# The fourth sample part ahead of the sixth slot's low halves, and the first output slot ahead of two pooling maps

## The reference, cut to what matters

```python
hn = _rmsnorm(h, norm1_g[l])
u = hn @ w_in[l]                      # 1024 -> 512 (pooling) + 2 * 512 (convolution)
pool_out, _ = _pool_mixer(...)        # windowed means of 2, 4, 8, 16 minus token, a 128x128 map for each of 4 groups, scale
conv_out, _ = _conv_module(...)       # GLU, depthwise convolution of 31 taps, LayerNorm, SiLU, 512x512 pointwise
h = h + jnp.concatenate([pool_out, conv_out], axis=-1) @ w_out[l]
hn = _rmsnorm(h, norm2_g[l])
h = h + (_swiglu(hn, ...) if l % 2 == 0 else _moe(hn, ...))
```

## Time and profile before

| | us |
|---|---|
| median of 3 runs (lowest, highest) | 1496.43 (1495.22, 1498.78) |
| the profiled execution | 1495.54 |
| its span, first to last instruction | 1493.8 |
| TensorE busy | 1461.5 |
| VectorE busy | 1182.0 |
| ScalarE busy | 915.1 |
| GpSimd busy | 202.1 |

### The profile page before, as it was taken

One profiled execution on the slowest core, in us unless ns is written; L12 is line 12 of the kernel. 1 busy time (PEld: TensorE's weight loads), 2 busy tenths in 40 slices (PEclk: granted clock), 3 DMA queues, 4 the chain that ended last, 5 costly groups with the idle time before them and its releaser, 6 DMA issues.

```text
span 1493.8 us, 21275 instructions
## 1 busy us (share of the span) xinstructions
PE 1461.5 (98%) x7895; PEld 1263.8 (85%) x7895; DVE 1182.0 (79%) x976; ACT 915.1 (61%) x740; POOL 202.1 (14%) x224
## 2 busy tenths in 40 slices
PE   8999999999999999999999999999999999999995
PEld 7879999999979977888888888888888888888884
DVE  4888655544686688888888888888888888888887
ACT  4253433333224587777777777777777777777773
POOL 1465000002344047500000000000000000000002
PEclk9999999999999999999999999999999999999997
DMA  7556996353284399999999999999999999999993
GB/s 203 159 188 207 334 286 198 95 173 113 64 253 161 119 364 400 384 395 377 390 364 385 386 361 384 379 379 382 374 382 371 376 385 361 382 388 370 382 379 113
DMA packets 249680, 453.56 MB, mean 304 GB/s; under 512 B 9605, under 2 KB 99781, under 8 KB 249631
## 3 DMA queue, kind: packets, MB, share of 16 engines
q1 hardware_dynamic: 245056, 442.33, 83.4%
q0 software_dynamic: 2960, 9.73, 2.0%
q10 hardware_dynamic: 1615, 0.85, 0.2%
HBM read 426.51 MB, written 26.37 MB: 303 GB/s over the span
## 4 chain that ended last, share of the span: by engine, by line
PE 66%; DVE 2%; ACT 1%; issue 1%; DVEq 0%; ACTq 0%
PE ps L1676 21%; PE ps L1674 21%; PE ps L1675 21%; PE ps L2044 2%; ACT w_hi L512 0%; PE ps L2034 0%; PE ps L2023 0%; DVE w_lo L517 0%; PE ps L1921 0%; PE ps L1757 0%; DVE yt L1656 0%; PE ps L2112 0%; DVE w_lo L1312 0%; PE ps L2113 0%; PE ps L1872 0%
## 5 line engine op out<-in xcount | busy, mean ns | idle before, releaser
L517 DVE TENSOR_TENSOR w_lo<-raw,w_hi 128x2048 fp32r<-128x2048 f32 x336 | 764.5, 2290 | 117.6 <-ACT w_hi L512 116.3
L512 ACT ACTIVATE w_hi<-raw 128x2048 fp32r<-128x2048 f32 x334 | 639.5, 1915 | 123.4 <-PE ps L1676 122.2
L1676 PE MATMUL ps<-w_hi,xg_lo 128*128 128x512 f32 x896 | 351.4, 392 | 0.0
L1674 PE MATMUL ps<-w_hi,xg_hi 128*128 128x512 f32 x896 | 350.9, 392 | 0.0
L1675 PE MATMUL ps<-w_lo,xg_hi 128*128 128x512 f32 x896 | 350.7, 391 | 0.0
L1675 PEld LDWEIGHTS ps<-w_lo,xg_hi 128*128 128x128 f32 x896 | 168.3, 188 | 37.2
L1674 PEld LDWEIGHTS ps<-w_hi,xg_hi 128*128 128x128 f32 x896 | 168.3, 188 | 36.7 <-DVE w_lo L517 0.2
L1676 PEld LDWEIGHTS ps<-w_hi,xg_lo 128*128 128x128 f32 x896 | 168.3, 188 | 36.1
L1674 PE MATMUL ps<-x_hi,w_hi 128*128 128x336 f32 x580 | 186.3, 321 | 5.9 <-DVE x_lo L1176 2.5
L1675 PE MATMUL ps<-x_lo,w_hi 128*128 128x336 f32 x580 | 183.6, 317 | 0.0
L1676 PE MATMUL ps<-x_hi,w_lo 128*128 128x336 f32 x580 | 182.9, 315 | 0.0
(11 more groups left out here) (283 smaller groups left out, 1576.1 us busy)
## 6 DMA issues: line engine op xcount, KB each, us to landing
raw<-in_moe_w_gate_dram SPq DMA_DIRECT2D x112, 1024.0 KB, 7.2
raw<-in_moe_w_up_dram SPq DMA_DIRECT2D x112, 1024.0 KB, 7.4
raw<-in_moe_w_down_dram SPq DMA_DIRECT2D x112, 1024.0 KB, 7.3
raw<-in_w_in_dram SPq DMA_DIRECT2D x11, 1024.0 KB, 5.2
raw<-in_ffn_w_gate_dram SPq DMA_DIRECT2D x11, 1024.0 KB, 6.0
raw<-in_ffn_w_up_dram SPq DMA_DIRECT2D x11, 1024.0 KB, 6.4
raw<-in_w_out_dram SPq DMA_DIRECT2D x8, 1024.0 KB, 7.7
obuf<-ones SPq DMA_DIRECT2D x15, 512.0 KB, 7.9
```

What stands on the lines that cost most here:

```text
L512: nc.scalar.activation(hi, r, ACT.Copy).then_inc(hi_done, 1)
L517: nc.vector.tensor_tensor(lo, r, hi.bitcast(F32), ALU.subtract).then_inc(lo_done, 1)
L1674: nc.tensor.matmul(out, a_hi, b_hi, start=start, stop=False)
L1676: return nc.tensor.matmul(out, a_lo, b_hi, start=False, stop=stop)
```

## The change

It has two parts, made in both mixer layers. On VectorE, both halves of the fourth tile's samples are done together, ahead of the sixth slot's low halves, and the low part of b+10 is no longer asked for ahead of the centring; the next request, for slots up to b+11, brings it along behind the centring. On TensorE, the first output slot is begun behind the pointwise tiles: both of its output tiles over six of the eight k, then the two last maps, and then the last two k for both tiles. The loop over output slots begins at the second.

```diff
--- before.py
+++ after.py
@@ -1287,7 +1287,7 @@
                 pool_in(4, 0)
                 conv_samples(2, (1,))
                 pool_in(4, 1)
-                conv_samples(3, (0,))
+                conv_samples(3)
 
                 def pooled_low(g):
 
@@ -1316,8 +1316,6 @@
                 low_half(0, pool_half_lo)
                 low_half(1, lo_done)
                 split_at[0] = n + 1
-                conv_samples(3, (1,))
-                split_to(b + S_POOL_W)
                 dve.wait_ge(sums_done, SUMS[("mean", l)] + 1)
                 for c in range(KC):
                     nc.vector.scalar_tensor_tensor(y[:, c, :], SUM_BANK, -1.0 / CW, y[:, c, :], ALU.mult, ALU.add
@@ -1908,8 +1906,24 @@
                                       k == 0, k == KC - 1)
                             if k == KC - 1:
                                 ins.then_inc(mm_done, 1)
+                split_ready(b + S_OUT)
+                w_hi_0, w_lo_0 = dense_slot(b + S_OUT, 256)
+                first_outs = [group(("wout", l, i)) for i in (0, 1)]
+
+                def first_part(ks):
+                    for k in ks:
+                        pe.wait_ge(evac, GROUP[("pool", l, k) if k < NG else ("pw", l, k - NG)] + 1)
+                        for i in (0, 1):
+                            cols = slice(P * i, P * (i + 1))
+                            ins = mm3(first_outs[i][:, 0:T], w_hi_0[:, k, cols], w_lo_0[:, k, cols], m_hi[:, k, :], m_lo[:, k, :],
+                                      k == M_ORDER[0], k == M_ORDER[-1])
+                            if k == M_ORDER[-1]:
+                                ins.then_inc(mm_done, 1)
+
+                first_part(M_ORDER[:2 + KC])
                 for g in POOL_ORDER[2:]:
                     pool_map(g)
+                first_part(M_ORDER[2 + KC:])
 
                 def logits(k):
 
@@ -1922,21 +1936,18 @@
                                                rwg[:, k, :], start=(k == 0 and t == 0), stop=(k == KD - 1 and t == 2))
                     return ins
 
-                for s in range(4):
+                for s in range(1, 4):
                     split_ready(b + S_OUT + s)
                     hi, lo = dense_slot(b + S_OUT + s, 256)
                     for i in (0, 1):
                         out = group(("wout", l, 2 * s + i))
                         for k in M_ORDER:
-                            if s == 0 and i == 0:
-
-                                pe.wait_ge(evac, GROUP[("pool", l, k) if k < NG else ("pw", l, k - NG)] + 1)
                             cols = slice(P * i, P * (i + 1))
                             ins = mm3(out[:, 0:T], hi[:, k, cols], lo[:, k, cols], m_hi[:, k, :], m_lo[:, k, :],
                                       k == M_ORDER[0], k == M_ORDER[-1])
                         ins.then_inc(mm_done, 1)
                     m = 2 * s + 1
-                    if l == 1 and s:
+                    if l == 1:
                         for k in (m - 3, m - 2):
                             logits(k)
                     if l == 1 and m == KD - 1:
```

## The result

The changed kernel takes 1500.91 us (median of 20 runs, 1497.90 to 1503.73), the kernel before 1496.15 beside it (20 runs). The ratio is 1.0031, with a 95% interval of 1.0025 to 1.0038, which is 3.7 to 5.7 us slower. The profiled execution has a span of 1499.2 us, where it was 1493.8.

The account below looks back on a forecast made before the run. TensorE, busy nearly the whole span, was taken as the bound. Two layers of 2.7 loss less 0.3 gain add 4.8 us to 1495.54, plus 0.89 to the median: 1501.2; own range 1499.2 to 1503.8, 8 in 10 within 1497.3 to 1504.6.

Parts of the forecast that it names:

- The mean's wait goes: Fourth tile's channel mean: samples ready at 78.2 to 79.4, so TensorE's 1.22 us wait per layer disappears.
- What part A is worth: Layer norm chain up to the spread matmul: between 1.22 us gain and 0.5 loss per layer, taken as 0.3 gain.
- About 1 us of idle back ahead of the spread matmul: Sign expected in the changed trace: the mean's idle time gone, about 1 us of it back at line 1706.
- Part B: Output stage: three TensorE waits per layer, about 0.85, 1.1 and 2.1 us; second output slot 2.7 us later.
- Rival 2: Output stage: second slot's low part ready when asked, both old stalls go, 5.2 us faster, 1491.2; chance 0.06.
- Later slots: Output slots behind the second: add nothing to the loss, as there is room to catch up.
- The sum: Both mixer layers: two times 2.7 - 0.3, 4.8 us slower, median 1501.2 us.
- Rival 3: TensorE's clock drops in the new gaps, costing 3.4 us once over dense matmuls: 1504.6; chance 0.12.

Follow-up runs that it names:

- Experiment 6: Kernel before with only the VectorE sample change, and pooled group 3's low part moved behind the variance arithmetic: ratio 0.9995 to the kernel before.
- experiment 5: Changed kernel with pooling and pointwise weight slots exchanged, second output slot's parts made ahead of the two maps' parts: ratio 0.9996 to the kernel before.
- part A alone: Kernel before with only the VectorE change (fourth tile's samples in one piece, earlier low-part request dropped), output stage as before: ratio 1.0000.

## Why the prediction was right

The forecast was 1501.2 and slower; measured was 1500.91. By its own steps, on the axis of the trace before (1.49 taken off):

- *The mean's wait goes:* right. Tile 3 was ready at 78.4 (78.2 to 79.4 forecast), the low halves ended at 82.2 (81.0 to 82.2), the centring began at 82.2 (81.8 to 82.2).
- *What part A is worth:* right in mechanism, a little off in size. From the centring to the variance arithmetic it was 6.48 us, where 5.5 to 6.5 was forecast, and the arithmetic began at 88.66, inside 87.3 to 88.7 and at its slow end; I took a gain of 0.3 per layer, and it is 0.0. The chain is the one that was bounded: the 512-column step moved behind the centring, the 2048-column subtraction ran beside GpSimd's last steps, and ScalarE's copy and VectorE's low part of group 3 came late behind them. Experiment 6 shows that the last link counts: with that low part out of the way the arithmetic starts 0.72 earlier. The Trainium skill, page "SBUF — State Buffer", section "Who interferes with whom", says that a VectorE instruction with two SBUF inputs and a GpSimd instruction that reads SBUF contend for a port that one of them holds exclusively; the 2.25 us that 64 columns took agree with it.
- *The clock behind the square sums* was no term of the sum. Had the arithmetic come 0.3 sooner, as I took it, TensorE at half clock would have held the spread matmul at 12.28 (experiment 6), and half of that gain would have been lost.
- *About 1 us of idle back ahead of the spread matmul:* not in the trace of the changed kernel, where the half clock filled the time; experiment 5's second layer shows it, at 1.54.
- *Part B:* right step by step, within 0.2 us, and closer at the end by luck. TensorE was to start the outputs at 103.9, and did at 104.01. The first map was to start at 109.44, and did at 109.63. From there to the last two k it was to take 2.03 us, and took 1.86, so that they started at 111.49 where 111.47 was forecast. ScalarE and VectorE came to the second slot 0.12 late, and the signal behind them took 0.05 where I had put 0.15: the slot started at 115.48 where 115.46 was forecast. Rival 2 fell with its own argument against it: the high part came behind the maps.
- *Later slots:* they added 0.1 us, where I had put nothing (from the first layer's second slot to the second layer's first mean 324.77 us, and 324.65 before).
- *The sum:* by distances +5.5 and not +4.8, since part A gave nothing. That the median came out at +4.8 is within its interval and luck, not a confirmation of the 0.3; stages that the change doesn't concern moved by more than that between the two profiles. The ends of the forecast's own range are a little wider than its terms give (2 x (2.7 - 1.22) and 2 x (3.0 + 0.5) make 1499.4 and 1503.4).
- *Rival 3* had the right effect in the wrong place, and not from the cause that it named. No new gap of the output stage, up to 1.88 us, dropped the clock (1.00 from 100 to 116). It dropped where there was no gap, behind the square sums, and cost nothing there because the arithmetic was as late.

## What to carry to other kernels

Work moved ahead of a step on one engine is paid for by what the other engines had queued behind that step: here two pooling maps of 0.46 us each, moved back by 5 to 7 us, held a weight buffer and ScalarE's and VectorE's whole queues, and the next slot came 2.7 us late. So when an instruction is moved, follow the buffers that it frees and the instructions that stand behind its result in program order, and fill a gap with just as much work as fits it: two k did here, six did not. A wait that is removed from a chain is won only if the chain's next link comes earlier too; measure from a fixed event to the next join, not the wait.

## What the runs showed of the hardware that was not expected

TensorE's clock fell to the lower level without any idle time ahead of it, behind the square sums (24 narrow matmul rows in 2.43 us, twelve matmuls in the code), for about 3.5 us. Five profiles have part A and the square sums in one piece, five have no part A; each has two layers and is one execution. With part A it came in eight layers of ten, without it in two of ten; why is open. With the sums tile by tile it came in four layers of four. Without part A an occurrence cost 1.4 us at the spread matmul; with part A alone, none, as the time was waited anyway.

The clock of stages that the change doesn't concern differed from one profile to the next, and by more time than part A was forecast to be worth: 1.49 us at the first projection, 2.9 in the routing stage.

A GpSimd instruction got in between two back-to-back instructions of VectorE: the two low halves took 2.50 us before and 3.48 after, 1.58 for the first and 1.98 for the second, and GpSimd's sum over 464 columns ended at 82.66, within the second:

```profile
80.84 1.82 POOL L701 TENSOR_TENSOR win_sum<-win_sum 128x464 f32<-128x464 f32 x1
```

```profile
81.77 1.98 DVE L1312 TENSOR_TENSOR w_lo<-raw,w_hi 128x1024 fp32r<-128x1024 f32 x1
```
